# Prompt attention of a hybrid decoder step: the query tiles taken from the last to the first

## The reference

```
def indexer_select(qi, wi, ki, qpos, topk):          # topk = 256
    s = relu(einsum('bthd,bsd->bths', qi, ki))
    score = einsum('bths,bth->bts', s, wi)
    score = where(arange(L) <= qpos, score, -inf)
    _, idx = top_k(score, topk)

def sparse_softmax(q, k_sel, v_sel, rel, valid, rel_bias):
    logits = einsum(q, k_sel) * ATT_DH ** -0.5 + rel_bias[t5_bucket(rel)]
    p = softmax(where(valid, logits, -inf))
    return einsum(p, v_sel)
```

## Time and profile before

| | before |
|---|---|
| median of 3 runs | 3218.36 us (3216.44 to 3218.62) |
| the profiled execution, time | 3222.45 us |
| the profiled execution, span | 3220.7 us |
| PE busy over the span | 2909.5 us (90%) |
| DVE busy over the span | 1486.0 us (46%) |
| the stage, first matmul to last copy | 735.51 to 838.67, 103.16 us |

### The profile page before, as it was taken

The page is one execution under the profiler, slowest core; times in us unless marked ns, Lnnn a source line. Parts: engine busy times, 40 slices in busy tenths (PEclk is TensorE's granted clock), DMA queues, the critical chain, the costliest instruction groups (busy, mean ns, idle before and its releaser), DMA issues. The chain is left out here.

```text
span 3220.7 us, 38878 instructions
## 1 busy us (share of the span) xinstructions
PE 2909.5 (90%) x16603; PEld 2670.1 (83%) x16603; DVE 1486.0 (46%) x1984; ACT 693.4 (22%) x1129; POOL 343.8 (11%) x320
## 2 busy tenths in 40 slices
PE   7989996729879899999999889958799999999998
PEld 6867775617549899999999889836599999999997
DVE  4699994778222423323323345348423332332334
ACT  4521220235311211111111132131312111111110
POOL 1043212502220100000000010025001000000000
PEclk8999998859989899999999989966699999999999
DMA  5032214043240211211121021100202112112111
GB/s 167 1 120 76 97 67 152 20 149 98 66 145 27 66 40 40 59 41 40 41 59 40 20 44 40 29 27 1 62 20 66 40 45 54 39 39 59 39 40 67
DMA packets 207485, 188.73 MB, mean 59 GB/s; under 512 B 18907, under 2 KB 160479, under 8 KB 207193
## 3 DMA queue, kind: packets, MB, share of 16 engines
q1 hardware_dynamic: 199777, 164.17, 16.9%
q0 software_dynamic: 7552, 22.29, 2.3%
HBM read 152.77 MB, written 33.50 MB: 58 GB/s over the span
## 5 line engine op out<-in xcount | busy, mean ns | idle before, releaser
L2002 DVE TENSOR_TENSOR xt<-ps,xt 128x1056 f32<-128x1056 f32 x176 | 221.1, 1256 | 203.5 <-PE ps L1786 203.5
L1786 PE MATMUL ps<-ffn_high,f_whG 128*128 128x352 f32 x1056 | 229.9, 326 | 11.9 <-DVE ffn_low L1716 7.8
L1786 PE MATMUL ps<-f_hidh,f_whD 128*128 128x352 f32 x1056 | 228.6, 325 | 9.9 <-DVE f_wlD L1981 9.9
L1786 PE MATMUL ps<-ffn_low,f_whG 128*128 128x352 f32 x1056 | 228.7, 325 | 0.0
L1786 PE MATMUL ps<-ffn_low,f_whU 128*128 128x352 f32 x1056 | 228.7, 324 | 0.0
L1786 PE MATMUL ps<-f_hidh,f_wlD 128*128 128x352 f32 x1056 | 228.6, 324 | 0.0
L1786 PE MATMUL ps<-f_hidl,f_whD 128*128 128x352 f32 x1056 | 228.0, 324 | 0.0
L1786 PE MATMUL ps<-ffn_high,f_whU 128*128 128x352 f32 x1056 | 227.8, 324 | 0.0
L1786 PE MATMUL ps<-ffn_high,f_wlG 128*128 128x352 f32 x1056 | 227.1, 323 | 0.0
L1786 PE MATMUL ps<-ffn_high,f_wlU 128*128 128x352 f32 x1056 | 226.6, 323 | 0.0
L765 PE MATMUL ps<-pe_wh,even_high 128*128 128x512 f32 (+1 forms) x504 | 201.3, 399 | 10.9 <-POOL pe_wl L821 10.9
(11 more groups left out here) (531 smaller groups left out, 4825.7 us busy)
## 6 DMA issues: line engine op xcount, KB each, us to landing
proj<-pe_out SPq DMA_DIRECT2D x56, 256.0 KB, 2.0
pe_w<-in_w_in_even_dram SPq DMA_DIRECT2D x6, 2048.0 KB, 8.4
ht_even<-in_w_gate_dram SPq DMA_DIRECT2D x22, 512.0 KB, 5.2
ht_even<-in_w_up_dram SPq DMA_DIRECT2D x22, 512.0 KB, 6.4
ht_even<-in_w_down_dram SPq DMA_DIRECT2D x22, 512.0 KB, 4.0
ht_odd<-in_w_gate_dram SPq DMA_DIRECT2D x22, 512.0 KB, 5.1
ht_odd<-in_w_up_dram SPq DMA_DIRECT2D x22, 512.0 KB, 6.3
ht_odd<-in_w_down_dram SPq DMA_DIRECT2D x22, 512.0 KB, 4.0
```

The costliest lines, as they stand in the source:

```text
L1786: last = pe.matmul(g.ps[0:out_rows, b0 + c, 0:THIRD], lhs, rhs[:, c * THIRD:(c + 1) * THIRD], start=(first and n == 0), stop=(final and n ...
L2002: dve.tensor_tensor(xv, g.ps[:, 3 * (m % 2):3 * (m % 2) + 3, 0:THIRD], xv, ALU.add).then_inc(added, 1)
```

## The change

One line. The list of units takes the tiles in falling order, heads in rising order within a tile as before:

```
-    units = [(t, h) for t in range(SMP) for h in range(H)]
+    units = [(t, h) for t in reversed(range(SMP)) for h in range(H)]
```

## The result

The changed kernel takes **3230.59 us** (median of 7 runs, 3224.47 to 3237.62), the kernel before 3220.01 beside it (7 runs, 3216.44 to 3223.76). The ratio is 1.0032 with a 95% interval of 1.0019 to 1.0045: slower by 10.6 us. With its seven runs the kernel before stands at 3220.01, where three had given 3218.36. The prediction said 3230.0, in 3224.5 to 3236.5, and slower with a chance of 0.88. The time held, and so did the mechanism in the stage itself. Two of its smaller sentences did not: the end is longer than was said, and so is the stage that follows.

What follows compares the result with a forecast made beforehand. PE was taken to bound the large tiles, with DVE nearly as slow beside rounds. Stage terms 59.9 + 51.0 + 3.7 = 114.6 against 103.16, +11.5 us, gave 3230 us, range 3224.5 to 3236.5.

Steps and rivals of the forecast that it cites:

- PE is the pace of the large tiles: Tiles 7 to 5, without rounds: PE sets the pace at 4.83, 4.28 and 3.74 us a unit, DVE needing half.
- The rival in which they shrink without the round: Large units speed up by up to 1.55 us in 12 units, -18.6 us, 3211 us; chance 0.04.
- The first stretch: Up to the mask of unit 14, no rounds, PE's pace: 59.9 us against 25.70 before, +34.2; bounds 58 and 61.
- slow clock: Start of the stage: 6.2 us at half speed with PE full, so 3.1 us lost again.
- The second stretch: Units 14 to 30, a round each, DVE slower than PE: 51.0 us against 66.35, -15.3; bounds 50 and 57.
- 0.5 for tile 4: Tile 4's units with rounds: 0.5 us added because PE is within 0.2 of DVE and waits for its scaling.
- The end: Unit 31, mask to copy, one chain through all engines: 3.7 us against 11.11, -7.4; bounds 2.5 and 5.
- The next stage as long as before: The following stage begins at half speed again for most of its first 12.33 us, its length unchanged.
- The clock rival: Second stretch, tiles 2 and 1: gaps drop PE to half clock, 6.8 us more, 3237 us; chance 0.14.
- Nearly no change: All three lower bounds together, perhaps with the next stage sooner at full clock: +2 to +7, about 3223 us; chance 0.08.

Runs made afterwards that it cites:

- e4: The kernel before (tiles rising) with the 17 rounds left out; 3218.72 us, ratio 0.9998 to the kernel before.
- e3: The changed kernel (tiles falling) with the 17 rounds left out; 3218.88 us, ratio 0.9999 to the kernel before.
- e7: The changed kernel with 20 transposes that nobody reads on PE at the next stage's start; 3230.5 us, ratio 1.0030 to the kernel before.
- e10: The changed kernel with the 20 unread transposes at the next stage's start, run a second time; 3229.78 us, ratio 1.0032 to the kernel before.
- e12: The changed kernel with the rounds beside units 7 to 23 instead of 14 to 30; 3225.82 us, ratio 1.0016 to the kernel before.
- e1: The changed kernel with the rounds beside units 0 to 16 instead of 14 to 30; 3222.52 us, ratio 1.0008 to the kernel before.
- e5: The changed kernel with the search of each of the 17 rounds run twice; ratio 1.0065 to the kernel before.
- e9: The changed kernel run once more, nothing altered; 3231.45 us, ratio 1.0036 to the kernel before.
- e2: The kernel before (tiles rising) with the rounds beside units 0 to 16 instead of 14 to 30; 3234.03 us, ratio 1.0048 to the kernel before.
- e6: The kernel before with the search of each of the 17 rounds run twice; ratio 1.0031 to the kernel before.

## Why the prediction held, point by point

- **PE is the pace of the large tiles** held. Large units on PE were 4.61, 4.06 and 3.52 us from mask to mask, the logits of one tile added to the values of the one before it in the list: 1.95 + 2.67, 1.74 + 2.33 and 1.53 + 2.00 by the prediction's own rows make 4.62, 4.07 and 3.53. The rival in which they shrink without the round is out: e4, without any, has the same PE-bound 62.73.
- **The first stretch**, 59.9, measured 59.80. Its slow clock at 0.95 of 59.80 us is 6.0 us at half speed, 3.0 lost (3.1 said), and with a full clock the same stretch takes 56.83 (e3, e7), which is the other terms' 56.8. But that loss is the execution's, not the stage's: e3 began at full speed with the same work, and the first stretch of one kernel ran from 56.83 (e7) to 59.80 (e10). That the sum was met to 0.1 is luck in this term.
- **The second stretch**, 51.0, measured 50.85. By tile it came out at 6.72 (two distances of tile 4), 12.87, 11.85, 11.04 and 8.37, where the prediction's terms give 6.70 + 0.5, 12.67, 11.87, 11.07 and 8.18. Its 0.5 for tile 4 was not needed; tiles 3 and 0 took 0.2 more each.
- **The end**, 3.7, measured 4.34. The row that it was taken from was the wrong one. Unit 0 ran at half clock with no units in front of it. Unit 31 has the values and copies of units 29 and 30 ahead of its own. That chain took 3.61 us at full clock (e3), 3.93 at 0.86 (e12), 4.34 at 0.64 and 4.89 at 0.50 (e7). The bounds, 2.5 and 5, held it.
- **"The next stage as long as before"** was wrong by 1.9 us. It takes 109.4 to 110.5 in after, e1, e3, e5 and e9, and 107.4 to 108.3 in before, e2, e4 and e6. That it would begin at half speed again was right, that it would leave it as soon was not. In after the clock was 0.50 for the whole of its first 12.33 us. A falling e12 has 108.41, so it is not the order as such. The pieces of after behind the restart:

```profile
854.00:862.00 8.00, 8.00 (x23) 4.87 (x24) 0.00 (x0) 1.45 (x3) 0.00 (x0) 0.50 0.00 0
862.00:864.00 2.00, 1.33 (x4) 0.32 (x3) 0.00 (x0) 0.90 (x2) 0.96 (x1) 0.50 0.00 0
864.00:866.00 2.00, 2.00 (x6) 0.57 (x5) 0.00 (x0) 0.00 (x0) 1.61 (x2) 0.50 0.49 152
866.00:868.00 2.00, 2.00 (x9) 0.54 (x8) 0.00 (x0) 0.00 (x0) 1.23 (x2) 0.81 0.77 203
```

  PE worked without a gap, stopped for 0.7 us while the clock was still 0.50, and worked for 3.6 us more before it had the full clock, at 866.8. In before the clock was full just ahead of the same stop:

```profile
843.00:851.00 8.00, 8.00 (x22) 4.86 (x23) 0.00 (x0) 1.19 (x3) 0.00 (x0) 0.51 0.00 0
851.00:852.00 1.00, 0.43 (x4) 0.19 (x2) 0.00 (x0) 1.00 (x2) 0.30 (x1) 1.00 0.00 0
```

  A stop at half speed is not enough for the long form, as e6 shows. There the clock was still 0.50 when the same stop came, full right after it, and the next stage was 107.35:

```profile
851.00:859.70 8.70, 8.70 (x24) 5.17 (x24) 0.00 (x0) 1.76 (x3) 0.00 (x0) 0.50 0.00 0
859.70:860.20 0.50, 0.01 (x1) 0.00 (x0) 0.00 (x0) 0.46 (x1) 0.22 (x1) 0.50 0.00 0
860.30:862.00 1.70, 1.62 (x6) 0.53 (x7) 0.00 (x0) 0.03 (x1) 1.39 (x2) 1.00 0.17 27
```

  Whether the stop has a part in putting the return off was not tried, and the cause of the +1.9 stays open.
- **The clock rival** (half speed in tiles 2 and 1, 3237) did not happen. PE was busy for 7.01 of 10 us in the pieces of tile 1, in short stretches with gaps, and the clock stayed at 1.00 up to 836.1. It fell to 0.50 there, 0.6 us ahead of tile 0's first mask (0.61 and 0.71 in the two pieces of 5 us). In tile 0 the prediction had it cost nothing: the distances, 2.67 and 2.62, are 2.61 and 2.54 in e9, where the clock stayed full, so it cost 0.14 us. The Trainium skill, "TensorE: Matmul & The Clock Gate", Part 1, says that activity lifts the slow level, which is the default. By that rule alone the time would have been the rival's 3237; the measured 1.00 beside such gaps decides against it here.
- **"Nearly no change"** did not happen, as its first half, all lower bounds at once, did not, and the next stage became slower rather than sooner warm.

In sum the stage came out at +11.83 for a forecast of +11.5, by terms that missed by -0.1, -0.15 and +0.64. The next stage's +1.9 was missed. The whole's +10.6, between 6.1 and 14.5, cannot tell 11.5 from the 13.7 that the two stages add up to. So the mechanism and the stage's sum are shown by the profiles, and that 3230.0 meets 3230.59 to 0.6 us is luck.

## What to carry to other kernels

Work that hides behind another engine has a place where it hides, and reversing a loop moves that place even if no instruction changes. Count what each step of the loop leaves free on the engine that does the hidden work, in the new order, and add up only what sticks out: here 26.4 us of rounds cost 3.6 us where the units grew from 4 to 8 key tiles and 13.7 where they shrank from 5 to 1. If the order has a reason of its own, move the hidden work along with the long steps, a few steps behind the start (e12's units 7 to 13 took seven rounds for some 0.6 us, and e1's first units stood still for 2.08 us).

## What the runs showed of the hardware that was not expected

- TensorE's granted clock at one and the same place differs between executions of one kernel: 1.00 and 0.50 in the state-space stage (4.5 us), and a first stretch of 56.83 to 59.80 us in the prompt's attention. Single profiles of one and the same code differ by that much.
- The clock held at 1.00 with PE busy for 7.01 of 10 us, in many short gaps, while a stage in the earlier trace rows with 13.88 of 20 us was granted 0.72. The busy share alone doesn't tell which level a stage gets.
- Twenty transposes that nobody reads, in a wait of some 4 us, took 3.5 to 5.6 us off the next stage in each of four profiles (104.94, 104.66, 103.83 and 104.43, against 110.05, 109.41 and 108.16), and nothing that can be measured off the whole.
